# Splitting the first layer normalisation: centring per token before the transpose, gain and shift per feature after it

## What is computed

```
def layer_norm(x, g, b):
    xf = x.astype(jnp.float32)
    mu = jnp.mean(xf, axis=-1, keepdims=True)
    var = jnp.mean(jnp.square(xf - mu), axis=-1, keepdims=True)
    return ((xf - mu) * lax.rsqrt(var + LN_EPS) * g + b).astype(x.dtype)

hp = layer_norm(x_prompt, ln_in_g, ln_in_b)
hs = layer_norm(x_sample, ln_in_g, ln_in_b)
for layer in range(DEPTH):
    # proj = x @ w_in + b_in, split in 13 parts; two attention branches y_a, y_b
    # merged = sigmoid(r_a) * (y_a @ w_proj_a) + sigmoid(r_b) * (y_b @ w_proj_b)
    x = layer_norm(ALPHA * x + merged @ w_out, ln_g, ln_b)
```

## Time and profile before

| | us |
|---|---|
| median of 3 runs | 1057.68 (1056.74 to 1057.71) |
| the profiled execution, its own time | 1056.88 |
| its span in the trace | 1055.1 |
| PE busy | 1003.9 (95%) |
| VectorE (DVE) busy | 606.0 (57%) |
| GpSimd (POOL) busy | 498.6 (47%) |
| ScalarE (ACT) busy | 480.1 (46%) |
| share of PE in the chain that ended last | 76% |
| share of DVE in it | 15% |

### The profile page before, as it was taken

One profiled execution on the slowest core, in us unless ns is written; L12 is line 12 of the kernel. 1 busy time (PEld: TensorE's weight loads), 2 busy tenths in 40 slices (PEclk: granted clock), 3 DMA queues, 4 the chain that ended last, 5 costly groups with the idle time before them and its releaser, 6 DMA issues.

```text
span 1055.1 us, 18633 instructions
## 1 busy us (share of the span) xinstructions
PE 1003.9 (95%) x7557; PEld 919.1 (87%) x7557; DVE 606.0 (57%) x1203; ACT 480.1 (46%) x824; POOL 498.6 (47%) x334
## 2 busy tenths in 40 slices
PE   1899999999999999999998999989999999999996
PEld 1789898878899999998777899977888999999975
DVE  6659997788983101101583899987898311100137
ACT  1355435667876322223124733466688542222210
POOL 2234455544564744445434174554455474445540
PEclk9999999999999999999999999999999999999999
DMA  6531453011112224323225223211111222352312
GB/s 198 192 102 46 146 165 126 2 41 41 41 41 81 80 81 161 100 81 120 91 68 195 76 91 113 82 58 42 41 41 42 72 65 80 100 184 81 106 55 90
DMA packets 70073, 95.44 MB, mean 90 GB/s; under 512 B 4458, under 2 KB 61252, under 8 KB 69348
## 3 DMA queue, kind: packets, MB, share of 16 engines
q1 hardware_dynamic: 66068, 82.68, 24.2%
q0 software_dynamic: 3488, 10.46, 2.9%
q10 hardware_dynamic: 432, 1.11, 0.3%
HBM read 79.46 MB, written 14.78 MB: 89 GB/s over the span
## 4 chain that ended last, share of the span: by engine, by line
PE 76%; DVE 15%; DMA 3%; issue 2%; ACT 2%; POOL 2%; SPq 0%; DVEq 0%; ACTq 0%; POOLq 0%
PE ps L514 35%; PE ps L861 10%; PE ps L812 10%; DVE attn L1346 3%; PE ps L727 3%; DVE top L1343 3%; PE ps L537 2%; PE ps L748 2%; PE ps L787 2%; PE ps L766 2%; PE ps L706 2%; DVE attn L1319 2%; DMA raw<-in_w_in 2%; DVE attn L1381 1%; DVE x_nat L1235 1%
## 5 line engine op out<-in xcount | busy, mean ns | idle before, releaser
L1566 POOL TENSOR_TENSOR w_lo<-raw,w_hi 128x1024 fp32r<-128x1024 f32 (+1 forms) x116 | 283.0, 2440 | 404.6 <-ACT w_hi L912 404.5
L514 PE MATMUL ps<-xT_hi,w_hi 128*128 128x288 f32 x864 | 256.1, 296 | 0.0
L514 PE MATMUL ps<-xT_hi,w_lo 128*128 128x288 f32 x864 | 254.5, 295 | 0.0
L514 PE MATMUL ps<-xT_lo,w_hi 128*128 128x288 f32 x864 | 254.5, 295 | 0.0
L912 ACT ACTIVATE w_hi<-raw 128x1024 fp32r<-128x1024 f32 (+1 forms) x116 | 121.2, 1046 | 107.2 <-PE ps L514 72.7
L1527 DVE TENSOR_TENSOR qy<-qy,ps 128x576 f32<-128x576 f32 x32 | 24.1, 754 | 253.8 <-PE ps L514 253.8
L514 PEld LDWEIGHTS ps<-xT_hi,w_hi 128*128 128x128 f32 x864 | 162.1, 188 | 1.3 <-issue 1.1
L514 PEld LDWEIGHTS ps<-xT_lo,w_hi 128*128 128x128 f32 x864 | 162.1, 188 | 0.0
L514 PEld LDWEIGHTS ps<-xT_hi,w_lo 128*128 128x128 f32 x864 | 162.0, 188 | 0.0
L961 ACT ACTIVATE qy<-ps,bias 128x576 f32<-128x576 f32 x34 | 25.2, 742 | 126.3 <-PE ps L514 126.2
L1657 POOL TENSOR_TENSOR attn<-attn 128x1024 f32<-128x1024 f32 (+1 forms) x24 | 54.2, 2259 | 59.2 <-DVE attn L1454 59.2
(11 more groups left out here) (202 smaller groups left out, 2300.3 us busy)
## 6 DMA issues: line engine op xcount, KB each, us to landing
raw<-in_w_in SPq DMA_DIRECT2D x44, 1024.0 KB, 5.2
raw<-in_w_out SPq DMA_DIRECT2D x8, 1024.0 KB, 5.0
x_kept<-x_nat SPq DMA_DIRECT2D x2, 2560.0 KB, 11.1
x_nat<-x_kept SPq DMA_DIRECT2D x2, 2560.0 KB, 11.2
raw<-in_w_proj_a SPq DMA_DIRECT2D x8, 512.0 KB, 3.5
raw<-in_w_proj_b SPq DMA_DIRECT2D x8, 512.0 KB, 4.7
x_nat<-in_x_prompt SPq DMA_DIRECT2D x4, 512.0 KB, 7.6
out<-stage POOLq DMA_DIRECT2D x8, 256.0 KB, 4.3
```

The source lines that it names most:

```text
L514: last = mm(out, a, b[:, HALF * half:HALF * (half + 1)], start=(k == 0 and i == 0), stop=(k == n - 1 and i == 2))
L1566: g.tensor_tensor(lo, src, hi.bitcast(f32), ALU.subtract).then_inc(s_lo, 1)
```

## The change

The first layer normalisation is computed in two parts. VectorE only centres and scales by rstd, token by token (`first_norm`), in an order that takes two tiles at a time. TensorE transposes the pair into 256 columns per block of features. ScalarE applies gain and shift there, where they are one number per partition, from PSUM into a new SBUF buffer `x_full` of five slots (`x_by_feature`), and writes hi from it (`x_hi`); VectorE writes lo from it (`first_x_rest`). For the sample's tile VectorE applies gain and shift (`sample_by_feature`). gain and shift come as 16 rows of 128 and are transposed by TensorE into `gb_T`. The parts of units 0 and 1 are 256 and 320 columns in the first layer. x spilled to memory is without gain and shift; `scale_and_shift_x` applies them on VectorE ahead of unit PR 6, from two broadcasts that GpSimd's queue fetches at the merge's beginning. `rest(0)` moves from GpSimd to VectorE (`first_rest`). TensorE gets dummy transposes (`keep_warm`). The transpose of b_in moves behind `front(1, 0)`; SP waits for tile 3 before weights chunk 1.

```diff
+FIRST_PAIR = 256
+        gb_rows = view(r0, 128)
+        x_full = view(o_v, 5, 512)
+        gain_in = stage[:, :, :].rearrange("p a n -> p (a n)")[:, 0:D]
+        shift_in = view(18432, D)
...
+            sp.wait_ge(s_xin[3], 16)
             weights(1, 0)
...
             pe.wait_ge(s_ident, 16)
-            pe.wait_ge(s_bias, 64 * DEPTH)
-            nc.tensor.transpose(ps[:, 0, 0:nb], bias_rows[0:nb, :], ident[0:nb, 0:nb]).then_inc(s_biasT, 1)
+            pe.wait_ge(s_gbr, 32)
+            nc.tensor.transpose(ps[:, 0, 0:16], gb_rows[0:16, :], ident[0:16, 0:16]).then_inc(s_gbt, 1)
+            def first_transposes(pair):
+                for t in (2 * pair, 2 * pair + 1):
+                    keep_warm(6)
+                    for b in range(4):
+                        i = 4 * pair + b
+                        if b % 2 == 0:
+                            pe.wait_ge((s_x0, s_x)[b // 2], t + 1)
+                        if pair and t % 2 == 0:
+                            pe.wait_ge(s_xf, i - 3)
+                        for k in (2 * b, 2 * b + 1):
+                            at = 256 * (k % 2) + 128 * (t % 2)
+                            last = nc.tensor.transpose(ps[:, 4 + b, at:at + 128], x_nat[:, t, 128 * k:128 * k + 128], ident)
+                        if t % 2:
+                            last.then_inc(s_xt, 1)
...
-                for t in range(4 if L == 0 else 0):
-                    x_transpose(L, t)
                 if L == 0:
-                    pe.wait_ge(s_biasall, 1)
+                    first_transposes(0)
+                    first_transposes(1)
+                    keep_warm(8)
+                    pe.wait_ge(s_gbT, 1)
                 front(0, 0)
                 x_transpose(L, 4)
                 front(1, 0)
+                if L == 0:
+                    pe.wait_ge(s_bias, 64 * DEPTH)
+                    nc.tensor.transpose(ps[:, 3, 0:nb], bias_rows[0:nb, :], ident[0:nb, 0:nb]).then_inc(s_biasT, 1)
                 front(0, 1)
...
+            def x_by_feature(i):
+                b = i % 4
+                act.wait_ge(s_xt, i + 1)
+                if i >= 5:
+                    act.wait_ge(s_xlo, i - 4)
+                for k in (2 * b, 2 * b + 1):
+                    at = 256 * (k % 2)
+                    last = act_f(x_full[:, i % 5, at:at + 256], ps[:, 4 + b, at:at + 256], ACT.Identity,
+                                 bias=gb_T[:, 8 + k:9 + k], scale=gb_T[:, k:k + 1])
+                last.then_inc(s_xf, 1)
...
+            def first_norm(t):
+                dve.wait_ge(s_std, t + 1)
+                v.reciprocal(rstd[:, t:t + 1], std[:, t:t + 1]).then_inc(s_rstd, 1)
+                dve.wait_ge(s_rstd, t + 1)
+                for half, signal in ((slice(0, 512), s_x0), (slice(512, D), s_x)):
+                    v.tensor_scalar(x_nat[:, t, half], x_nat[:, t, half], mean_var[:, t, 0:1], rstd[:, t:t + 1],
+                                    ALU.subtract, ALU.mult).then_inc(signal, 1)
+            def sample_by_feature(kk):
+                i = 8 + kk
+                dve.wait_ge(s_gbT, 1)
+                dve.wait_ge(s_xt, i + 1)
+                dve.wait_ge(s_xlo, i - 4)
+                for k in range(4):
+                    f = 4 * kk + k
+                    last = v.tensor_scalar(x_full[:, i % 5, DEC * k:DEC * k + DEC], ps[:, 4 + i % 4, DEC * k:DEC * k + DEC],
+                                           gb_T[:, f:f + 1], gb_T[:, 8 + f:9 + f], ALU.mult, ALU.add)
+                last.then_inc(s_xf_s, 1)
...
+                def scale_and_shift_x():
+                    dve.wait_ge(s_back, 16)
+                    dve.wait_ge(s_gb_in, 32)
+                    for t in range(5):
+                        row = x_nat[:, t, :]
+                        v.tensor_tensor(row, row, gain_in, ALU.mult).then_inc(s_x_in, 1)
+                    for t in range(5):
+                        row = x_nat[:, t, :]
+                        dve.wait_ge(s_x_in, t + 1)
+                        v.tensor_tensor(row, row, shift_in, ALU.add).then_inc(s_x_in, 1)
+                    dve.wait_ge(s_x_in, 10)
                 for m in range(8):
+                    if L == 0 and m == 6:
+                        scale_and_shift_x()
...
-                rest(0)
+                if L:
+                    rest(0)
+                pool.wait_ge(s_lo, L * NU + 2)
                 rest(1)
...
+                if L == 0:
+                    for slot in range(2):
+                        pool.wait_ge(s_ka_st[slot], 64)
+                    g.dma_start(gain_in, A["ln_in_g"].partition_broadcast(128)).then_inc(s_gb_in, 16)
+                    g.dma_start(shift_in, A["ln_in_b"].partition_broadcast(128)).then_inc(s_gb_in, 16)
```

More of the change, by code:

```diff
@@ L403, in y_head, with first_views @@
                                  mybir.ActivationFunctionType.Copy).then_inc(s_yhi, 1)
+        def first_views(i):
+            if i < 8:
+                pair, b = divmod(i, 4)
+                ks, cols = slice(2 * b, 2 * b + 2), slice(256 * pair, 256 * pair + 256)
+            else:
+                ks, cols = slice(4 * (i - 8), 4 * (i - 8) + 4), slice(SEQ, TOK)
+            n = (ks.stop - ks.start) * (cols.stop - cols.start)
+            return (x_full[:, i % 5, 0:n].rearrange("p (k n) -> p k n", k=ks.stop - ks.start), xT_hi[:, ks, cols])
         @block.sync
@@ L486, in x_transpose @@
                     if i >= 4:
[L487 removed]
+                        pe.wait_ge(s_xlo if L else s_xf, L * 10 + i - 3)
                     elif L:
@@ L912, in head_of, with x_hi, first_stds, first_norm_front @@
                 act_f(hi, src, ACT.Copy).then_inc(s_hi, 1)
+            def x_by_feature(i):
[8 more added lines that the diff above has]
+                last.then_inc(s_xf, 1)
+            def x_hi(i):
+                if i < 8:
+                    act.wait_ge(s_xf, i + 1)
+                else:
+                    act.wait_ge(s_xf_s, i - 7)
+                src, hi = first_views(i)
+                act_f(hi, src, ACT.Copy).then_inc(s_xhi, 1)
+            def first_stds(tiles):
+                for t in tiles:
+                    act.wait_ge(s_mv, t + 1)
+                    act_f(std[:, t:t + 1], mean_var[:, t, 1:2], ACT.Sqrt, bias=one_eps[:, 1:2]).then_inc(s_std, 1)
+            def first_norm_front():
+                first_stds((0, 1))
+                x_by_feature(0)
+                x_by_feature(1)
+                x_hi(0)
+                first_stds((2, 3))
+                x_by_feature(2)
+                x_hi(1)
+                head_of(0, 0)
+                x_by_feature(3)
+                x_hi(2)
+                x_hi(3)
+                head_of(0, 1)
+                x_by_feature(4)
+                x_by_feature(5)
+                x_hi(4)
+                first_stds((4,))
+                x_by_feature(6)
+                x_hi(5)
+                x_by_feature(7)
+                x_hi(6)
+                x_hi(7)
+                x_hi(8)
+                x_hi(9)
             def norm_front(L):
@@ L1247, in x_rest, with first_stats @@
                                     ALU.subtract).then_inc(s_xlo, 1)
-            dve.wait_ge(s_const_b, 4)
-            for t in range(5):
+            def first_stats(t):
                 dve.wait_ge(s_xin[t], 16)
@@ new lines, in first_x_rest @@
+            def first_x_rest(i):
+                dve.wait_ge(s_xhi, i + 1)
+                src, hi = first_views(i)
+                if i < 8:
+                    pair, b = divmod(i, 4)
+                    lo = xT_lo[:, 2 * b:2 * b + 2, 256 * pair:256 * pair + 256]
+                else:
+                    lo = xT_lo[:, 4 * (i - 8):4 * (i - 8) + 4, SEQ:TOK]
+                v.tensor_tensor(lo, src, hi.bitcast(f32), ALU.subtract).then_inc(s_xlo, 1)
+            def sample_by_feature(kk):
[8 more added lines that the diff above has]
+                last.then_inc(s_xf_s, 1)
@@ L1261, in _ @@
+            first_stats(4)
+            first_x_rest(2)
+            first_rest(0)
+            first_x_rest(3)
+            first_norm(4)
+            first_x_rest(4)
+            sample_by_feature(0)
+            first_x_rest(5)
+            sample_by_feature(1)
+            first_x_rest(6)
+            first_x_rest(7)
+            first_x_rest(8)
+            first_x_rest(9)
             for L in range(DEPTH):
```

65 lines of the change are left out of this document (48 added, 17 removed).

## The result

| | before | after |
|---|---|---|
| median, us | 1057.23 (1056.74 to 1057.71, 4 runs) | 1044.19 (1043.43 to 1044.97, 4 runs) |
| the profiled execution, its own time | 1056.88 | 1044.97 |
| its span in the trace | 1055.1 | 1043.0 |
| PE busy | 1003.9 | 1007.2 |
| DVE / ACT / POOL busy | 606.0 / 480.1 / 498.6 | 618.9 / 489.5 / 500.1 |

The change is faster: ratio 0.9881, 95% interval 0.9868 to 0.9893. It gains 13.0 us by the medians (1057.23 − 1044.19); 11.7 were forecast (1057.2 − 1045.5, or 12.2 by the marks).

What follows compares the result with a forecast made beforehand. VectorE's opening, statistics of all five tiles before any pass, was taken to delay unit 2. Its start moving from 50.92 to 38.7 gives 12.2 us, the merge adding nothing: execution 1044.7, median 1045.5 us, range 1041.0 to 1050.5.

Steps and rivals of the forecast that it cites:

- the marks: First layer, first matmul of unit 2: its start moves from 50.92 to 38.7, a gain of 12.2 us.
- The first steps: Opening: small rows in at 6.4, first pair normalised at 9.9, roots end at 14.1, second pair normalised at 16.1 us.
- Transfers: Opening: two broadcasts, 1 MB, leave the start; tile 0 counted at 4.8 instead of 5.33, small rows in at 6.4 us.
- The shared port: Before unit 0: GpSimd's w_lo of unit 1 holds VectorE's lo subtractions; 1.5 us charged, between 0 and 2.2.
- VectorE sets the start: Unit 0: VectorE ready at 20.9 without a hold, TensorE through at 18.0; start at 22.4 with the hold.
- unit 0 limited by something other than VectorE: Unit 0's start: listed sign that the prediction is wrong, which had VectorE setting that start; no size given.
- Unit 0 to unit 2: First layer: upper clock, matmuls 0.12 apart, TensorE waits for VectorE until 30.8, unit 2 starts at 38.7 us.
- rival 2: Before unit 3, first layer: the weights' transfer becomes the wait; landing 4 us later costs 2.4, 1047.9 us; chance 0.10.
- Rival 1: Unit 0: TensorE's clock drops after standing 4.4 us; 24 matmuls take 5.1 instead of 2.8, 1047.8 us; chance 0.20.
- Rival 3: Merge: GpSimd starves behind VectorE's ten gain and shift operations, w_lo comes 4.7 us late, 1050.2 us; chance 0.10.
- Rival 4: Merge: each of the ten operations is held 3.0 us, unit PR 6 waits 14.9, 1060.4 us; chance 0.02.
- Rival 5: Opening: ScalarE stands at weights chunk 1 or small rows come late; unit 2 unmoved, 1057.7 us; chance 0.02.

Runs made afterwards that it cites:

- the statistics run: Changed kernel with VectorE taking the statistics of all five tiles first, as the kernel before did, then normalising pair 0; 1048.92 us, ratio 0.9921.
- the execution of 2240.43 us: Profiled execution of the first run of the changed kernel without its 32 dummy transposes; that run's median was 1045.94 us, ratio 0.9888.

## Why the prediction was right, point by point

**The first steps.** Small rows in at 6.4: 6.58. First pair normalised 9.9: 10.05. Roots 14.1: 14.3. Second pair normalised 16.1: 16.6, as a pass of 512 columns costs 0.46 from start to start and not 0.42, and a scaling of 256 columns with gain and shift from PSUM about 0.46 and not the 0.33 of the plain evacuation it was costed by. VectorE ready for unit 0 at 20.9 without a hold: 21.08.

**Transfers.** I gave the removed megabyte a part in the early tiles (4.8 instead of 5.33). Tile 0 came at 4.95, but with the broadcasts back it came at 4.90: the time was right and the reason wrong. The small rows came at 6.58, and at 6.43 with the broadcasts behind them; what they would cost with the broadcasts ahead of them no run shows. The value of the early statistics came from VectorE's order, which the statistics run shows.

**The shared port.** This step failed. I placed GpSimd's w_lo of unit 1 beside the lo subtractions and charged 1.5 us; GpSimd waits there for VectorE's w_lo of unit 0 (`s_lo`, in the diff), so its 2.77 us fell on the sample tile's pass, 1.52 instead of 1.00, behind which VectorE had 0.61 us of idle to take it up. The price itself was right: 2.1 us where the run with w_lo on GpSimd brings the two together, within the 0 to 2.2 given. The Trainium skill (SBUF — State Buffer, section "SBUF: two separate sides") has a VectorE instruction with two SBUF inputs and a GpSimd instruction that reads SBUF shut each other out; the 3.41 us instead of 1.29 agree with it, as do the ten operations of the merge (two SBUF inputs each) with their 19.4 us.

**What sets unit 0.** "VectorE sets the start" failed too, and "unit 0 limited by something other than VectorE" was on the prediction's own list of signs that it is wrong. I had TensorE through with its transposes and dummies at 18.0. TensorE's waits for ScalarE, 14 dummies and eight transposes, most of them at the lower clock, ended at 21.68, 3.7 us later, VectorE at 21.08. Where the clock stayed up, in the second run of the changed kernel, the first matmul waited 0.97 us for VectorE. So either can be the later one, and my 22.4 was 0.7 too late: the hold of 1.5 that did not come, less 0.6 of TensorE and 0.2 of VectorE.

**Unit 0 to unit 2.** Upper clock, matmuls 0.12 apart: right. The second parts at 30.8: 29.92, waiting 1.35 for VectorE as forecast. Unit 2 at 38.7: **38.11**. The 12.2 us became 12.8. That the first trace gained 12.1 us in all, so near to the 12.2, is luck in part: the 12.8 of unit 2 are 12.5 at unit 3, 10.7 behind the slow stretch at 96 us and 12.1 behind the second layer's quicker chunk, and of these steps only the one to unit 3 (rival 2) was foreseen.

**Rival 1** (low clock in unit 0) is what the kernel without dummies does, by 1.3 us at the second parts where I gave 2.3, as its unit 0 starts a microsecond earlier. The Trainium skill (TensorE: Matmul & The Clock Gate, Part 1) has the clock fall when the engine stands idle; the granted clock of 0.50 from 17 us on, behind 2.22 and then 1.42 us of standing, before and within the second pair's transposes, agrees. The premise of this rival, 4.4 us of standing before unit 0, did not come about: TensorE came late itself.

**Rival 2** (the weights' transfer) came about, and small: its chunk landed at 41.26 where I had 39.9 (23.4 + 0.4 + 16.1), TensorE was ready at 44.57 (45.1 forecast) and stood 0.30 us. **Rival 3**: GpSimd's subtractions took at most 2.90 beside the ten operations, and no gap of TensorE came. **Rival 4**: the ten took 1.9 each, 19.4 us together and above the 12 to 16 given as a sign, but under the 4.2 from which it would decide. **Rival 5**: the first root stands at 7.09.

**What was not in the sum.** The second layer's chunk landed in 14.4 to 14.5 us in six of the seven traces of the changed order that have this wait, and in 15.83 in the seventh; before it took 16.06, in the one trace of before that has it. The transfers beside it are the same by count and size. Whether the change makes them quicker, or before has quick executions too, one trace does not tell, and the reason stays open. In the second trace of the changed kernel this chunk is why 11.9 us at unit 3 of the first layer are 13.0 at the same unit of the second (568.51 − 555.52). The other term is the slow stretch behind 96 us, 1.5 us in the first trace and none in the second.

## What to carry to other kernels

A normalisation ahead of a transpose can be cut where its numbers change from per token to per feature; one part of what pays is that the first tiles leave VectorE before it has looked at the last ones: undone, it cost 6.4 us at unit 0 and 4.7 of the 13.0 in the whole. Where two engines hold each other up, as VectorE and GpSimd do here, move the second engine's work behind the first's critical row, even if the first has to take over a small piece of it: with 0.75 us of subtraction VectorE was spared 2.1 of hold, and unit 2 came 0.96 earlier. When a long wait is gone, read each queue again for a copy that nobody waits for and that stands ahead of a transfer which somebody does: that was 2 us in both kernels.

## What the runs showed of the hardware that was not expected

**The clock can fall on a busy TensorE.** After the eight small matmuls at 93.26, of 32 rows by 384 columns, the dense unit took 8.09 us:

```profile
96.23 0.44 PE L558 MATMUL ps<-xT_lo,w_hi 128*128 128x288 f32 x1
96.47 0.44 PE L558 MATMUL ps<-xT_hi,w_lo 128*128 128x288 f32 x1
```

```profile
95.00:100.00 5.00, 5.00 (x23) 4.32 (x22) 4.79 (x10) 2.23 (x5) 4.03 (x3) 0.66 0.37 120
```

TensorE is busy 5.00 of 5.00 us, and the granted clock is 0.66. The same loss, 1.5 us, stands behind this group or the next one like it in five of eleven traced executions of the changed order and in neither of the two of before that were traced. Two traces are too few to say that the kernel before is free of it. Which executions it meets follows no edit: of two traces of the changed kernel itself, one has it. Differences here of under 1.5 us between single groups of runs rest on little for that reason.

**The record of the clock does not say when it was low before it first fell.** In the kernel before, 288 columns in 0.24 us are the 1.2 GHz level while the granted clock reads 1.00; in the run without dummies the same level reads 0.50. The distance between starts tells it in both. In the execution of 2240.43 us the record is of no help at all: it has a clock of 1.00, and the first 24 matmuls of 256 columns took 7.15 us, 0.30 from start to start.
